# Compression's first layer as one product of 128 stationary columns (high and low rows side by side), with the second query chunk in front of it

## The reference, cut to what matters

```python
h = rms_norm(x, mix_norm_pre[l])
proj = h @ w_in[l]
q, kc, vc, ksl, vsl, kw, vw, gt, pin, u, v = jnp.split(proj, IN_SPLITS, axis=-1)
...
# for keys and for values: windows of CMP_LEN = 32 rows plus cmp_pos, flattened to 2048 numbers
# hidden = gelu(window @ cmp_w1 + cmp_b1)      2048 -> 128, the first layer
# compressed = hidden @ cmp_w2 + cmp_b2        128 -> 64, the second layer
```

## Time and profile before

| | |
|---|---|
| median of 3 runs | 926.4 us (926.29, 926.4, 930.9) |
| the profiled execution | 926.42 us, of which the span of the trace is 924.7 us |
| PE, busy share of the span | 99% |
| DVE, ACT, POOL | 71%, 58%, 13% |
| mean granted TensorE clock | 0.999 of full speed |
| weight chunks | 288 transfers of 512 KB |

### The profile page before, as it was taken

How to read it: one execution, slowest core, us unless ns; L and a number is a source line. 1 busy time by engine, 2 the same in 40 slices (tenths; PEclk the granted TensorE clock), 3 DMA queues, 4 the chain that set the end, 5 groups by cost and what they waited for, 6 DMA issues and landing times.

```text
span 924.7 us, 19117 instructions
## 1 busy us (share of the span) xinstructions
PE 911.5 (99%) x6977; PEld 855.9 (93%) x6977; DVE 657.0 (71%) x1117; ACT 533.2 (58%) x905; POOL 124.7 (13%) x121
## 2 busy tenths in 40 slices
PE   8999999999999999999999999999999999999997
PEld 7998889998999999889999999999999998888886
DVE  4898877555899997447877777776577566767743
ACT  5868677445776676446444444444454566666643
POOL 2200011000056656000111111101010000000000
PEclk9999999999999999999999999999999999999999
DMA  8853425535456655662655555565465544455551
GB/s 282 288 176 118 135 89 165 181 115 169 132 166 195 202 203 181 229 184 97 199 176 177 171 178 172 172 201 175 145 198 182 168 147 135 162 173 160 182 195 55
DMA packets 45076, 157.91 MB, mean 171 GB/s; under 512 B 6068, under 2 KB 7220, under 8 KB 44765
## 3 DMA queue, kind: packets, MB, share of 16 engines
q1 hardware_dynamic: 44524, 155.56, 51.8%
q0 software_dynamic: 496, 1.59, 0.6%
HBM read 156.06 MB, written 1.06 MB: 170 GB/s over the span
## 4 chain that ended last, share of the span: by engine, by line
PE 93%; DVE 4%; ACT 2%; issue 1%; DMA 1%; SPq 0%; DVEq 0%; ACTq 0%
PE acc L1294 13%; PE acc L1295 13%; PE acc L1296 13%; PE scores L1294 6%; PE scores L1295 6%; PE scores L1296 5%; PE acc L1249 4%; PE acc L1248 4%; PE acc L1247 4%; PE scores L1249 2%; PE scores L1248 2%; PE scores L1247 2%; PE outs L1249 2%; PE outs L1248 2%; PE outs L1247 2%; PE acc L1369 1%
## 5 line engine op out<-in xcount | busy, mean ns | idle before, releaser
L1849 DVE TENSOR_TENSOR w_lo<-raw,w_hi 128x1024 fp32r<-128x1024 f32 x288 | 354.0, 1235 | 97.9 <-ACT w_hi L650 97.4
L650 ACT ACTIVATE w_hi<-raw 128x1024 fp32r<-128x1024 f32 x288 | 302.4, 1056 | 151.2 <-PE acc L1296 63.8
L1294 PE MATMUL acc<-XH,w_hi 128*128 128x256 f32 (+1 forms) x624 | 178.2, 286 | 0.6 <-DVE XL L1955 0.6
L1295 PE MATMUL acc<-XL,w_hi 128*128 128x256 f32 (+1 forms) x624 | 175.8, 282 | 0.0
L1296 PE MATMUL acc<-XH,w_lo 128*128 128x256 f32 (+1 forms) x624 | 175.8, 282 | 0.0
L1294 PEld LDWEIGHTS acc<-XH,w_hi 128*128 128x128 f32 x624 | 117.4, 188 | 3.1 <-issue 2.6
L1294 PE MATMUL scores<-XH,w_hi 128*128 128x272 f32 (+1 forms) x424 | 120.1, 283 | 0.0
L1296 PE MATMUL scores<-XH,w_lo 128*128 128x272 f32 (+1 forms) x424 | 119.7, 282 | 0.0
L1295 PE MATMUL scores<-XL,w_hi 128*128 128x272 f32 (+1 forms) x424 | 119.7, 282 | 0.0
L1295 PEld LDWEIGHTS acc<-XL,w_hi 128*128 128x128 f32 x624 | 117.5, 188 | 0.1
L1296 PEld LDWEIGHTS acc<-XH,w_lo 128*128 128x128 f32 x624 | 117.4, 188 | 0.0
(11 more groups left out here) (533 smaller groups left out, 1795.8 us busy)
## 6 DMA issues: line engine op xcount, KB each, us to landing
raw<-weights SPq DMA_DIRECT2D x288, 512.0 KB, 3.5
cst<-params SPq DMA_DIRECT2D x1, 1080.5 KB, 10.6
XR<-x_t SPq DMA_DIRECT2D x2, 512.0 KB, 6.6
Y<-mem_t SPq DMA_DIRECT2D x1, 1024.0 KB, 9.6
AR<-bias_rows POOLq DMA_DIRECT2D x4, 256.0 KB, 5.8
out<-AR SPq DMA_DIRECT2D x2, 512.0 KB, 2.7
AR<-final_gain POOLq DMA_DIRECT2D x1, 512.0 KB, 6.5
cst<-params SPq DMA_DIRECT2D x1, 114.5 KB, 3.1
```

The costliest lines, as they stand in the source:

```text
L650: nc.scalar.activation(w_hi[:, n % SLOTS, :], raw[:, n % SLOTS, :], ACT.Copy).then_inc(hi_ready, 1)
L1294: nc.tensor.matmul(o, wh, h, start=start, stop=False)
L1295: nc.tensor.matmul(o, wh, l, start=False, stop=False)
L1849: V.tensor_tensor(w_lo[:, s, :], raw[:, s, :], w_hi[:, s, :].bitcast(F32), ALU.subtract).then_inc(lo_ready, 1)
```

## The change: what it does

The high and the low rows of a window block are laid side by side in AH (16 blocks of 2 x 64 columns, line 225 of the new file). One product with all 128 columns as stationary operand then gives high-by-weight in partitions 0 to 63 and low-by-weight in 64 to 127. Two products a step (with `w_hi` and with `w_lo`) take the place of three. The two halves are added where the result is turned: the two transposes become four products with a slice of the identity (two for each bank, the second adding to the first).

The second query chunk becomes chunk 7 and stands in front of the first layer, whose chunks become 8 to 11; the spreading of the memory's factor moves between the two pairs of the first layer; query 3 moves ahead of the second layer. DVE, ACT and POOL are reordered to suit.

```diff
-_LAYOUT = [("kc", 1), ("vc", 1), ("vsw", 2), ("ks", 1), ("kw", 1), ("qa", 1), ("cmp", 4), ("qb", 3), ("gates", 1), ("sgu_v", 2), ("sgu_u", 2),
+_LAYOUT = [("kc", 1), ("vc", 1), ("vsw", 2), ("ks", 1), ("kw", 1), ("qa", 2), ("cmp", 4), ("qb", 2), ("gates", 1), ("sgu_v", 2), ("sgu_u", 2),
...
+        RF_hl = AH[:, 2048:4096].rearrange("p (a b c) -> p a b c", a=16, b=2)
...
-            for j, done in enumerate((CHUNK["qa"], CHUNK["cmp"] + 1, CHUNK["cmp"] + 3, CHUNK["qb"])):
+            for j, done in enumerate((CHUNK["qa"], CHUNK["qa"] + 1, CHUNK["cmp"] + 1, CHUNK["cmp"] + 3)):
...
-            nc.scalar.activation(AH[:, 2048:3072], RF[:, :, :, :, :].rearrange("p a b c d -> p (a b c d)"), ACT.Copy).then_inc(rf_hi, 1)
+            nc.scalar.activation(RF_hl[:, :, 0, :], RF[:, :, :, :, :].rearrange("p a b c d -> p a (b c d)"), ACT.Copy).then_inc(rf_hi, 1)
...
-            ahead(CHUNK["cmp"] + 1)
+            ahead(CHUNK["cmp"])
             swap(0, "ks")
             swap(1, "kw")
-            for c in range(2, 4):
-                ahead(CHUNK["cmp"] + c)
-            ahead(query(1)[0])
             act.wait_ge(rstd_spread, NORM_MEM + 1)
             nc.scalar.activation(rstd_m[:, 0:S], spread_mem(), ACT.Copy).then_inc(mem_rstd, 1)
+            for c in range(1, 4):
+                ahead(CHUNK["cmp"] + c)
...
+            chunk(*query(1), xh, xl, S)
             pe.wait_ge(cmp_in, 1)
             for c in range(2):
                 n, t = CHUNK["cmp"] + 2 * c, TILE["cmp"]
                 begin(n + 1, t, c == 0)
-                o = acc(t)[0:64, 0:S].rearrange("p (r c) -> p r c", r=2)
+                o = acc(t)[:, 0:S].rearrange("p (r c) -> p r c", r=2)
                 for k in range(KT):
                     j, cols = KT * c + k, slice(k * P, (k + 1) * P)
-                    rows = slice(2048 + 64 * j, 2048 + 64 * (j + 1))
-                    nc.tensor.matmul(o, AH[:, rows], slots(w_hi, n, cols), start=(j == 0), stop=False)
-                    nc.tensor.matmul(o, AL[:, rows], slots(w_hi, n, cols), start=False, stop=False)
-                    last = nc.tensor.matmul(o, AH[:, rows], slots(w_lo, n, cols), start=False, stop=(j == 15))
+                    both = RF_hl[:, j, :, :].rearrange("p a b -> p (a b)")
+                    nc.tensor.matmul(o, both, slots(w_hi, n, cols), start=(j == 0), stop=False)
+                    last = nc.tensor.matmul(o, both, slots(w_lo, n, cols), start=False, stop=(j == 15))
                 last.then_inc(chunk_done, 2)
-            pe.wait_ge(bias_copied, 1)
-            chunk(*query(1), xh, xl, S, between=lambda: spread_rstd(NORM_MEM, S, spread_mem()))
+                if c == 0:
+                    pe.wait_ge(bias_copied, 1)
+                    spread_rstd(NORM_MEM, S, spread_mem())
+            chunk(*query(2), xh, xl, S)
 
             wait_evacuated(pe, TILE["cmp"])
             pe.wait_ge(root_ready, 1)
-            nc.tensor.transpose(OB[1][:, 0:32], ch[0:32, 0:P], ident[0:32, 0:32])
-            nc.tensor.transpose(OB[0][:, 0:32], ch[32:64, P:S], ident[32:64, 32:64]).then_inc(cmp_hidden, 1)
-            chunk(*query(2), xh, xl, S)
+            for bank, cols, at in ((OB[1], slice(0, P), 0), (OB[0], slice(P, S), 32)):
+                for part in range(2):
+                    last = nc.tensor.matmul(bank[:, 0:32], ch[:, cols], ident[:, 64 * part + at:64 * part + at + 32],
+                                            start=(part == 0), stop=(part == 1))
+            last.then_inc(cmp_hidden, 1)
+            chunk(*query(3), xh, xl, S)
...
             last.then_inc(cmp_out, 1)
-            chunk(*query(3), xh, xl, S)
             chunk(CHUNK["gates"], TILE["gates"], xh, xl, S)
...
-            V.tensor_tensor(AL[:, 2048:3072], rf, AH[:, 2048:3072].bitcast(F32), ALU.subtract).then_inc(cmp_in, 1)
-            lo(8)
+            V.tensor_tensor(RF_hl[:, :, 1, :], rf, RF_hl[:, :, 0, :].bitcast(F32), ALU.subtract).then_inc(cmp_in, 1)
...
             keep_keys(1, "kw", acc(TILE["kw"]))
+            lo(8)
             lo(9)
             lo(10)
...
             keep_query(0)
             invert_root(NORM_MEM, S)
+            keep_query(1)
             n, t = CHUNK["cmp"], TILE["cmp"]
-            ahead(n + 1)
-            ahead(n + 2)
+            for c in range(3):
+                ahead(n + c)
             wait_chunk(dve, n + 3)
-            freed(V.tensor_copy(ch[0:64, :], acc(t)[0:64, 0:S]), t)
-            ahead(n + 3)
+            freed(V.tensor_copy(ch, acc(t)[:, 0:S]), t)
...
-            keep_query(1)
-            ahead(query(1)[0])
             dve.wait_ge(mem_rstd, 1)
             normalise_mem(0, 3)
+            ahead(n + 3)
             keep_query(2)
             ahead(query(2)[0])
+            keep_query(3)
...
             last.then_inc(cmp_kv, 2)
-            keep_query(3)
             ahead(query(3)[0])
             normalise_mem(3, KT).then_inc(mem_normed, 1)
```

More of the change, by code:

```diff
@@ L101, in query @@
 def query(j):
-    return (CHUNK["qa"], TILE["qa"]) if j == 0 else (CHUNK["qb"] + j - 1, TILE["qb"] + j - 1)
+    return (CHUNK["qa"] + j, TILE["qa"] + j) if j < 2 else (CHUNK["qb"] + j - 2, TILE["qb"] + j - 2)
 def span(k, w):
@@ L1991, in _ @@
             dve.wait_ge(rf_hi, 1)
-            rf = RF[:, :, :, :, :].rearrange("p a b c d -> p (a b c d)")
-            V.tensor_tensor(AL[:, 2048:3072], rf, AH[:, 2048:3072].bitcast(F32), ALU.subtract).then_inc(cmp_in, 1)
-            lo(8)
+            rf = RF[:, :, :, :, :].rearrange("p a b c d -> p a (b c d)")
+            V.tensor_tensor(RF_hl[:, :, 1, :], rf, RF_hl[:, :, 0, :].bitcast(F32), ALU.subtract).then_inc(cmp_in, 1)
             def keep_keys(j, name, src):
@@ L2628, in _pack_weights @@
     queries = [_tiles(np, q, p) for p in pairs]
-    parts += queries[0:1] + pairs_of("cmp", hidden) + queries[1:4] + [narrow(gt, ar(24))] + pairs_of("sgu_v", lin(v)) + lin(u) + lin(pin)
+    parts += queries[0:2] + pairs_of("cmp", hidden) + queries[2:4] + [narrow(gt, ar(24))] + pairs_of("sgu_v", lin(v)) + lin(u) + lin(pin)
     mv = lin(a["w_mv"][0])
```

## The result

| | before | after |
|---|---|---|
| median of the runs | 926.55 us (22 runs) | 929.2 us (22 runs) |
| profiled execution / its span | 926.42 / 924.7 us | 928.72 / 927.0 us |

The ratio is 1.0029, 95% interval [1.0023, 1.0035]: 2.65 us slower on the medians, 2.3 in the profiled pair. The forecast was +1.1 (927.5).

A forecast was written before the change was run, and what follows sets the result against it. PE is 99% busy, but DVE's chain is level with it at the turned gates (55.24 us). Terms gave -0.43 on PE, but DVE's lateness there +1.1 on 926.4: 927.5 us, 8-in-10 range 925.3 to 929.2.

The forecast's parts named there:

- the last term of the sum: At the turned gates, PE waits 1.3 us for DVE's late chain; the point shifts +1.1 us, carried to the end.
- The products, −1.87: First layer on PE: 32 products instead of 48 at an unchanged 0.117 us each, 1.87 us less.
- The old wait, −0.44: Ahead of the first layer: PE's wait of 0.44 us for acc0 goes, as query 1 follows the sums of squares.
- The turned result, +0.67: Turning the first layer's result: eight float32 instructions take 0.93 us instead of 0.26, 0.67 us more on PE.
- acc1 freed late, +0.19: Start of the first layer: PE waits for DVE to take query 0 out of acc1, 0.19 us late.
- Query 2 waits, +1.02: Behind the first layer: PE waits 1.02 us for chunk 12's low part, starting query 2 at 42.72 instead of 41.70.
- Rival D: Query 2 does not wait but DVE's tail counts: +0.1, 926.5 us; chance 0.20.
- The low rows, 0: Making the low rows in place with a pitch of 128 was taken to cost 0.
- DVE's tail: DVE's steps behind the second layer's results, up to the gates, end late: turned gates at 56.32 against 55.24, +1.1 us.
- Rival B: PE's saving arrives, with no hold by DVE's tail and no wait of query 2: 1.45 us gained, 925.0; chance 0.15.
- Rival C: Weight transfer for chunk 15's high part lands late: up to 1.9 us more, 929.4; chance 0.15 together with dear turning.
- the forecast's own sign of being wrong: One of its listed signs: a difference between the kernels that first opens behind 57 us.

The follow-up runs named there:

- e1: The changed kernel with six small filling products of constants on PE ahead of the turned gates; 927.91 us, +1.24, ratio 1.0010.
- e3: The kernel before, with one weight chunk's low part moved ahead of DVE's taking-out of the gates, so that PE waits there; 929.41 us, +2.74.
- e6: The changed kernel's order of chunks with the old 48 products of 64 columns and the old two transposes; 929.08 us, +3.1, ratio 1.0032.
- e2: The changed kernel with four of DVE's last five memory scalings moved right behind the third query chunk; 925.98 us, −0.69, ratio 0.9988.
- e5: The kernel of e3 with the six filling products of e1 in the wait; 927.6 us, +1.64, ratio 1.0021.
- e8: The kernel of e7 with the old 48 products of 64 columns and the two transposes; 926.04 us, +0.08, ratio 1.0000.
- e7: The kernel of e2 with ACT splitting chunks 12 and 13 between its other steps; 924.65 us, −1.31, ratio 0.9987.
- e9: The changed kernel with ACT's order of e7, all five last scalings behind the third query chunk and later low parts on DVE; 925.04 us, −1.05.
- e4: The kernel before with only the 32 products of 128 columns and the four-product turning, no chunk moved; 926.71 us, +0.04, ratio 1.0005.

## Why the prediction was wrong

The mechanism was the one forecast; the step that failed is the last term of the sum, "then 1.3 of waiting at the turned gates, where DVE's chain is late: +1.1". It priced the wait at its own length and put what follows it at nothing ("a shift there is carried to the end"). The runs show a second price, 1.7 us of full clock lost behind the wait. Where a time of day stands beside a forecast one, the 0.60 is added.

- *The products, −1.87.* Right in the main. 0.12 us each with 128 stationary columns (36.58 to 36.70), no dearer than with 64. From 36.39 to 38.38, where the spreading starts, and from 39.19 to 41.19, one step behind the last, they took 3.99 in place of 5.62, so 1.63 less: each pair has a slow first product. The Trainium skill's rule on the load ("TensorE: Matmul & The Clock Gate", LDWEIGHTS) would have made a step 0.17 if nothing hid the load, an estimate from that page. The trace agrees on how much longer the loads got, from 134 to 192 ns (medians of PEld in L1428 and L1429), though both are some 80 ns above what the rule gives; but they ran beside the stream.
- *The old wait, −0.44.* Right, query 1 starts at once behind the sums of squares.
- *The turned result, +0.67.* 0.81 us in place of 0.93: +0.55.
- *acc1 freed late, +0.19.* There, but smaller. DVE has taken out query 0 at 36.84 (forecast 36.93), and the first layer starts 0.15 behind that, at 36.99 (37.07). The last product of query 1 started 0.21 us before it instead of 0.12, so 0.09 were lost; the list of waits does not show them, since the pipelined product before covers them.
- *Query 2 waits, +1.02.* The wait is there, for DVE's `lo` as forecast: 0.71 by the row, 0.87 by the distance of the starts (41.19 to 42.06). Query 2 starts at 42.66 (42.72). Rival D is out.
- *The low rows, 0.* Right: the subtraction took 1.58 us before and after (L1993, L1997), though the prediction has it at 1.2, which is the time of a `lo`.
- *DVE's tail.* Forecast at the turned gates: 56.32, PE waiting 1.3 us. Measured: 55.63 + 0.60 = 56.23 and 1.54 us. That is +0.99 against 55.24. The tail was 0.09 earlier than forecast, and PE, at 54.69 in place of 54.99, 0.30 earlier. Rival B fell to this.
- *Rival C.* `hi` of chunk 15 did not wait for its transfer (46.76 in the trace, directly behind the gelus). `hi` of 16 did, for 0.74 us, but DVE reached its `lo` only later. Transfers were not the cause; that the total stands near rival C's 929.4 is chance.
- *What was missing: the clock.* Eight score products at 1.29 in place of 0.93 us, chunk products at 0.21 in place of 0.12, back to normal at about 60; the forecast's own sign of being wrong, a difference that first opens behind 57 us, came close to it. 1.70 us by the windows, 1.53 by the heads' turns. 0.99 + 1.53 = 2.52, against 2.65 on the medians. e1 takes this term away and leaves the rest (+1.24); e3 makes it in the kernel before (+2.74), without any part of the change.

The other executions point the same way. A fall of 1.7 us would bring the mean granted clock of a span of 927 us down by 0.002. Of the 22 of the changed kernel one has a mean of 1.000, and it is the fastest, 927.73 us, about where e1 stands; of the six of e6 one has 1.000, 927.14 us, against 928.93 and more for the others. They have no trace, so this is a sign and no proof. If it holds, the same wait does not bring the clock down in every execution.

What stays open is small. The two terms leave 0.1 us of the medians' 2.65. In the profiled pair the changed kernel goes from 1.92 us behind at 109 us to 2.3 at the end, and e1 from 0.54 to 1.1, with the clock at 1.00 in both. Followed by DVE's 288 `lo`, the distance of the changed kernel changes in small steps: 1.91 at 111 us (times of before), 1.81 at 185, 2.09 at 287, 2.30 at 517, 2.31 at 910. The step of about 0.25 between 222 and 287 us is there in e2, e3, e5, e6 and e8 too, but not in e1, e7 and e9, so it isn't the change's. No wait of the size of the whole stands there, and no run was made for it. With the 0.60 of the start, the pair would be 2.9 apart; single executions differ by such amounts, as the sums of squares start anywhere from 32.34 to 32.94 in the eleven traces.

One could have asked about the clock beforehand: the kernel before already issues filling products (`keep_warm`) at some waits of PE. The forecast did not ask what the new wait would do to the granted clock, and none of the rows of before that were read told the size.

## What to carry to other kernels

When a step makes PE wait where it did not, price two things: the length of the wait, and the stretch behind it at the lower clock; read the granted clock in windows of 1 us, since a mean over the span hides both. Ahead of a saving on the engine that is 99% busy, follow the chain to the other engines: where the point at which PE meets them is already level, a saving on one side alone is lost. The products alone gave nothing (e4, +0.04), the repaired order alone gave nothing (e8, +0.08), and both together gave 1.31 us (e7). And compare before and after at the same event in each trace, not at the same microsecond.

## What the runs showed of the hardware

- The granted clock fell to half behind waits of 1.19 (e3), 1.52 (e6) and 1.54 us (after). All three came directly behind the compressed scores (16 float32 instructions of 32 moving columns) and ahead of more small products. It did not fall behind the waits of 0.71 us (after) and 0.45 us (e7), nor behind the 1.15 us in e9, which came directly behind full chunk products. 1.15 and 1.19 us are too close to tell whether the length decides, or the small products around the wait; neither was tried by itself. Each fall took 1.7 us of full clock.
- Six 128x128 float32 products in the wait, 1.58 us of work, kept the clock at 1.00 (e1, e5), and did not delay the gates: counted from the sums of squares they start at 23.29 us in e1 and in the changed kernel alike, and at 23.51 in e5 against 23.60 in e3.
- fp32r products of 256 moving columns took 0.12 us from start to start with 64 and with 128 stationary columns alike, so with high and low rows side by side two products did the work of three at no price in the stream (3.99 us for the layer in place of 5.62). The loads of the weights took 134 ns with 64 columns and 192 with 128, beside the stream.
